# Masks, scan and PSUM banks in a two-kind transformer kernel: one mask product per head and scores first, one masked scan per direction, paired banks

## The reference, cut to what matters

```python
# first kind: RWKV-7 time mix (8 heads of 64), a pool branch, gates, feed-forward
def step(state, inp):                      # 512 steps
    r_t, w_t, k_t, v_t, kk_t, a_t = inp
    sk = jnp.einsum('bhvk,bhk->bhv', state, kk_t)
    state = (state * w_t[:, :, None, :] - sk[..., None] * (a_t * kk_t)[:, :, None, :]
             + v_t[..., None] * k_t[:, :, None, :])
    return state, jnp.einsum('bhvk,bhk->bhv', state, r_t)
mixed = br_gate[:, :, 0] * (y_a @ proj_a[l]) + br_gate[:, :, 1] * (y_b @ proj_b[l])
x = x + gt1 * (mixed @ w_out[l])
# second kind: gated linear attention in both directions (4 heads, keys 128, values 256) ...
cum = jnp.cumsum(la, axis=3)               # la = log_sigmoid(...) / 16, per chunk
q_dec, k_intra = q * jnp.exp(cum), k * jnp.exp(-cum)
# ... beside softmax attention (8 query heads, 2 key heads of 128), gates, feed-forward
pr = jax.nn.softmax(sc, axis=-1)
mixed = jax.nn.sigmoid(gate_a) * branch_a + jax.nn.sigmoid(gate_b) * branch_b
```

## Time and profile before

| | us |
|---|---|
| median of 3 runs (3934.14 to 3939.48) | 3936.67 |
| the profiled execution | 3938.62 |
| its span, first to last instruction | 3936.8 |
| PE busy | 3727.2 (95%) |
| PEld (weight loads) busy | 3017.7 (77%) |
| DVE busy | 1827.7 (46%) |
| ACT busy | 842.1 (21%) |
| POOL busy | 2269.6 (58%) |

### The profile page before, as it was taken

One profiled execution on the slowest core, in us unless ns is written; L12 is line 12 of the kernel. 1 busy time (PEld: TensorE's weight loads), 2 busy tenths in 40 slices (PEclk: granted clock), 3 DMA queues, 4 the chain that ended last, 5 costly groups with the idle time before them and its releaser, 6 DMA issues.

```text
span 3936.8 us, 53124 instructions
## 1 busy us (share of the span) xinstructions
PE 3727.2 (95%) x21300; PEld 3017.7 (77%) x21300; DVE 1827.7 (46%) x2494; ACT 842.1 (21%) x1318; POOL 2269.6 (58%) x2218
## 2 busy tenths in 40 slices
PE   5999999999999899999899999999998999999997
PEld 4777678887777678887777677888787776778886
DVE  5644653244754652125543554523465435453325
ACT  3321110005121110003321532000243225220002
POOL 4523767785523677774446356777644453567773
PEclk9999999999999999998999999999989999999998
DMA  4223445342223443332223132333322331333332
GB/s 184 83 79 107 140 144 145 118 145 73 71 79 103 142 145 109 97 97 67 65 73 121 52 99 83 97 97 97 96 62 62 95 95 57 105 83 97 97 98 65
DMA packets 192196, 386.09 MB, mean 98 GB/s; under 512 B 21456, under 2 KB 21584, under 8 KB 190288
## 3 DMA queue, kind: packets, MB, share of 16 engines
q1 hardware_dynamic: 169776, 338.24, 29.1%
q10 hardware_dynamic: 22176, 44.45, 3.2%
HBM read 361.64 MB, written 20.97 MB: 97 GB/s over the span
## 4 chain that ended last, share of the span: by engine, by line
PE 83%; DVE 10%; ACT 4%; DMA 1%; issue 1%; ACTq 0%; SPq 0%; DVEq 0%
PE psum L415 17%; PE psum L417 17%; PE psum L416 17%; PE psum L487 3%; PE psum L489 2%; PE psum L488 2%; PE psum L509 2%; PE psum L970 1%; DVE units L1849 1%; PE psum L945 1%; PE psum L603 1%; PE psum L462 1%; PE psum L593 1%; PE psum L807 1%; PE psum L809 1%
## 5 line engine op out<-in xcount | busy, mean ns | idle before, releaser
L2249 POOL TENSOR_SCALAR w_hi<-raw 128x512 fp32r<-128x512 f32 x1082 | 747.0, 690 | 1523.4 <-DMA raw<-weight_chunks 1520.5
L2251 POOL TENSOR_TENSOR w_lo<-raw,w_hi 128x512 fp32r<-128x512 f32 x1082 | 1486.7, 1374 | 90.2
L415 PE MATMUL psum<-in_hi,w_hi 128*128 128x512 f32 x1920 | 761.7, 397 | 2.9 <-ACT mg L1545 1.3
L416 PE MATMUL psum<-in_lo,w_hi 128*128 128x512 f32 x1920 | 749.3, 390 | 0.0
L417 PE MATMUL psum<-in_hi,w_lo 128*128 128x512 f32 x1920 | 749.2, 390 | 0.0
L415 PEld LDWEIGHTS psum<-in_hi,w_hi 128*128 128x128 f32 x1920 | 361.9, 188 | 90.1 <-issue 11.1
L416 PEld LDWEIGHTS psum<-in_lo,w_hi 128*128 128x128 f32 x1920 | 361.8, 188 | 80.3 <-issue 6.2
L417 PEld LDWEIGHTS psum<-in_hi,w_lo 128*128 128x128 f32 x1920 | 361.5, 188 | 76.1
L487 PE MATMUL psum<-in_hi,w_hi 128*128 128x512 f32 x576 | 255.6, 444 | 20.0 <-ACT nt L1108 10.0
L488 PE MATMUL psum<-in_lo,w_hi 128*128 128x512 f32 x576 | 227.2, 394 | 0.0
L489 PE MATMUL psum<-in_hi,w_lo 128*128 128x512 f32 x576 | 227.0, 394 | 0.0
(11 more groups left out here) (430 smaller groups left out, 6703.7 us busy)
## 6 DMA issues: line engine op xcount, KB each, us to landing
raw<-weight_chunks SPq DMA_DIRECT2D x1082, 256.0 KB, 2.6
ada_col<-ada_slabs SPq DMA_DIRECT2D x80, 512.0 KB, 4.1
spill<-gate_st ACTq DMA_DIRECT2D x56, 256.0 KB, 2.8
ada_at<-ada_slabs SPq DMA_DIRECT2D x8, 1024.0 KB, 15.8
gin<-spill ACTq DMA_DIRECT2D x32, 256.0 KB, 3.2
mgs<-spill ACTq DMA_DIRECT2D x32, 256.0 KB, 2.9
sml<-small ACTq DMA_DIRECT2D x4, 1024.0 KB, 5.6
spill<-nt ACTq DMA_DIRECT2D x16, 256.0 KB, 2.6
```

What stands on the lines that cost most here:

```text
L415: pe.matmul(bank[:], wh, hi[:, i, :], start=(i == 0), stop=False)
L416: pe.matmul(bank[:], wh, lo[:, i, :], start=False, stop=False)
L2249: ts(w_hi[:, slot, :], raw[:, slot, :], 1.0, 1.0, ALU.mult, ALU.mult).then_inc(sem("chunk_hi"), 1)
L2251: ins = tt(w_lo[:, slot, :], raw[:, slot, :], w_hi[:, slot, :].bitcast(F32), ALU.subtract)
```

## The change

- **Recurrence.** The scores come first in a chunk; the transposes `tok` 0, 1, 2 come in levels 2, 3, 4, behind the filler block. VectorE masks all 512 columns of a head in one product and computes `mt` for each half of the partitions from `units` directly; ScalarE copies the diagonal blocks to `ac`. Fillers: 0, 2, 2, 4 blocks behind the four pairs of scores in place of 6 behind all, and 1 behind `inv_t`.
- **Decays.** One scan of 512 tokens per head and direction, with a mask `keep2` of ones that is zero at the first token of each chunk. The middle value is subtracted from the scan's result directly; the exclusive sum of the backward direction is a subtraction shifted by one token and a column for the first token. `mid` and the two memsets go.
- **Banks.** Each bank has one count of uses. In both stages of the second kind of block (decays and heads; attention) projections use banks 0 and 1 ("lin2") and fillers banks 2 and 3 ("bg2"); `p2a`, `p2b` and all the rest use "lin" as before. In `gla_core` the fillers before the heads are 8, 2, 2, 8 in place of 2, 2, 2, 8.

```diff
+FILL_SCORE = (0, 2, 2, 4)
+FILL_CORE = (8, 2, 2, 8)
+        keep2 = ar("keep2", 2, [P, T])
-        mid = [ar(f"mid{i}", 94 + i / 32, [P, NCH]) for i in range(2)]
-        BANKS = {"lin": (0, 3), "bg": (3, 1), "aux": (4, 4)}
+        BANKS = {"lin": (0, 1, 2), "bg": (3,), "aux": (4, 5, 6, 7), "lin2": (0, 1), "bg2": (2, 3)}
+        uses_of = {}
...
             def begin(name, pool, order=None):
-                n = used[pool]
-                first, banks = BANKS[pool]
-                b, uses = first + n % banks, n // banks
+                b = BANKS[pool][used[pool] % len(BANKS[pool])]
+                uses = uses_of.get(b, 0)
+                uses_of[b] = uses + 1
...  (TensorE, wkv_chunk)
-                for i, src in enumerate((b_f, k_f, v_f)):
+                def token_rows(i):
...
+                pe.wait_ge(sem("wkv_in"), count("wkv_in", l))
                 for d in range(RT):
                     names = [("score", l, c, 2 * d + i) for i in range(2)]
...
+                    fill(FILL_SCORE[d])
-                fill(6)
...  (behind inv_t)
+                fill(1)
...
                     fill(2 if v == 1 else 1)
+                    if 2 <= v < 5:
+                        token_rows(v - 2)
                     pe.wait_ge(*moved(("am", l, c, v)))
...  (TensorE, block2)
-                side_jobs([(("g2a", l, m), "w_in2", l, N_GA + m) for m in range(DT)], "bg")
+                side_jobs([(("g2a", l, m), "w_in2", l, N_GA + m) for m in range(DT)], "bg2")
+                lane[0] = "lin2"
...  (ScalarE, wkv_chunk)
+                    gates_before(("score", l, c, NH - 1), gate_st)
+                    act.wait_ge(*moved(("score", l, c, NH - 1)))
+                    for k in range(2):
+                        rows = slice(HB * k, HB * k + HB)
+                        af(ac[rows, :, :], units[rows, :, 0, rows], ACT.Copy).then_inc(sem("diag_ready"), 1)
...  (VectorE, wkv_chunk)
-                    for i in range(2):
-                        ins = tt(units[:, h, 2 * i:2 * i + 2, :],
-                                 bank[:, 256 * i:256 * i + 256].rearrange("p (a t) -> p a t", a=2), pair, ALU.mult)
+                    tt(units[:, h, :, :].rearrange("p (j a) t -> p j (a t)", j=2),
+                       bank[:].rearrange("p (j t) -> p j t", j=2), pair, ALU.mult).then_inc(bank_read(job), 1)
...
-                    dve.tensor_copy(ac[rows, :, :], units[rows, :, 0, rows]).then_inc(sem("vector_step"), 1)
+                    tt(mt[rows, :, :], units[rows, :, 0, rows], compact(0, rows), ALU.mult).then_inc(sem("vector_step"), 1)
-                tt(mt[:], ac[:], compact(0), ALU.mult).then_inc(sem("vector_step"), 1)
...  (VectorE, gla_decay)
-                    for c in range(NCH):
-                        dve.tensor_tensor_scan(ln[h][i][:, c, :], kst[:, K_ONES, :], la[i][:, c, :], 0.0,
+                    ins = dve.tensor_tensor_scan(flat, keep2[:], flat, 0.0, ALU.mult, ALU.add)
+                    at = HB - 1 - i
+                    ins = tt(ln[h][i][:, :, i:P], la[i][:, :, 0:P - i],
+                             la[i][:, :, at:at + 1].to_broadcast([P, NCH, P - i]), ALU.subtract)
...
+                        ts(ln[h][1][:, :, 0], la[1][:, :, at], -1.0, None, ALU.mult).then_inc(sem("vector_step"), 1)
+                        ins = tt(dsc[h][1][:, 0:n], la[1][:, 0:n, P - 1], la[1][:, 0:n, at], ALU.subtract)
+                        ins = tt(dsc[h][1][:, 0:n], dsc[h][1][:, 0:n], la[1][:, 1:NCH, at], ALU.add)
```

More of the change, by code:

```diff
@@ L280, in emit @@
         jobs = {}
-        used = {"lin": 0, "bg": 0, "aux": 0}
+        used = {pool: 0 for pool in ("lin", "bg", "aux", "lin2", "bg2")}
         ranks = {"lin": 0, "bg": 0, "aux": 0, "late": 0}
-        BANKS = {"lin": (0, 3), "bg": (3, 1), "aux": (4, 4)}
+        BANKS = {"lin": (0, 1, 2), "bg": (3,), "aux": (4, 5, 6, 7), "lin2": (0, 1), "bg2": (2, 3)}
+        uses_of = {}
         closed = {}
@@ L320, in moved, with compact @@
             return bank_read(job), turn(job)
-        def compact(i):
+        def compact(i, rows=slice(0, P)):
             o = (K_HALF + i // 2) * P + i % 2 * HB
-            return kst[:].rearrange("p k t -> p (k t)")[:, o:o + HB].unsqueeze(1).to_broadcast([P, NH, HB])
+            part = kst[:].rearrange("p k t -> p (k t)")[rows, o:o + HB]
+            return part.unsqueeze(1).to_broadcast([rows.stop - rows.start, NH, HB])
         def half(t, b, second):
@@ L406, in linear @@
             def linear(name, blocks, hi, lo, ready):
-                bank = begin(name, "lin")
+                bank = begin(name, lane[0], "lin")
                 for i, desc in enumerate(blocks):
@@ L802, in token_major @@
                     ts_ = slice(t * P, (t + 1) * P)
-                    bank = begin(name + (t,), "lin")
+                    bank = begin(name + (t,), lane[0], "lin")
                     for k in range(DT):
@@ L838, in gla_core @@
                 v = gv[h % 2]
-                fill((2, 2, 2, 8)[h])
+                fill(FILL_CORE[h])
                 pe.wait_ge(sem("qd_ready"), count("qd_ready", (l, h)))
@@ L925, in block2 @@
                 fill(DT * DT)
+                lane[0] = "lin"
                 for m in range(DT):
@@ L928, in block2 @@
                                hi=go_hi, lo=go_lo)
-                side_jobs([(("g2b", l, m), "w_in2", l, N_GB + m) for m in range(DT)], "bg")
+                side_jobs([(("g2b", l, m), "w_in2", l, N_GB + m) for m in range(DT)], "bg2")
+                lane[0] = "lin2"
                 for i in range(KVH):
@@ L1214, in block1 @@
                 for c in range(NCH):
[L1215 to L1223, removed]
-                    flat = lambda t: t[:].rearrange("p h t -> p (h t)")
+                    flat = lambda t: t[:].rearrange("p h t -> p (h t)")
+                    gates_before(("score", l, c, NH - 1), gate_st)
[3 more added lines that the diff above has]
+                        af(ac[rows, :, :], units[rows, :, 0, rows], ACT.Copy).then_inc(sem("diag_ready"), 1)
+                        act.wait_ge(sem("diag_ready"), passed("diag_ready", (l, c)))
                     job = ("inv_t", l, c)
-                    gates_before(job, gate_st)
                     act.wait_ge(*done(job))
@@ L1235, in block1 @@
                         act.wait_ge(bank_read(job), turn(job))
+                        if 2 <= v < 5:
+                            job = ("tok", l, c, v - 2)
+                            act.wait_ge(*done(job))
+                            af(tok[v - 2][:], bank_of(job)[:], ACT.Copy).then_inc(bank_read(job), 1)
+                            act.wait_ge(bank_read(job), turn(job))
                     low, high = slice(0, HB), slice(HB, P)
@@ L1841, in wkv_chunk @@
             def wkv_chunk(l, c):
-                pair = kst[:, K_STRICT:K_INCL + 1, :]
+                pair = kst[:, K_STRICT:K_INCL + 1, :].rearrange("p a t -> p (a t)").unsqueeze(1).to_broadcast([P, 2, 2 * P])
                 for h in range(NH):
@@ L1869, in level_part @@
                     dve.wait_ge(sem("bm_ready"), passed("bm_ready", (l, c, v)))
+                dve.wait_ge(sem("diag_ready"), count("diag_ready", (l, c)))
                 level_part(1)
@@ L2117, in block2 @@
                 normed_inputs(("m1", l), cols_of(l, "g_mix_pre"))
+                for part, value in ((keep2[:], 1.0), (by_chunk(keep2[:])[:, :, 0:1], 0.0)):
+                    dve.memset(part, value).then_inc(sem("vector_step"), 1)
+                    dve.wait_ge(sem("vector_step"), passed("vector_step"))
                 for h in range(GH):
```

45 lines of the change are left out of this document (12 added, 33 removed).

## The result

The changed kernel takes 3910.7 us (median of 4 runs, 3909.2 to 3919.7) against 3937.3 of before (4 runs); the ratio is 0.9946 (0.9933 to 0.9958). By the medians that is 26.6 us faster where 49.7 were forecast, and 1.7 us outside the range. The ratio on record makes it 21 us; I can't say why the two differ. By the runs listed for this pair, what they gain on it would be 3 to 5 us smaller. The two profiled executions stand at spans of 3909.2 and 3936.8, 27.6 apart; the table splits that by TensorE's marks at the ends of the stages.

What follows compares the result with a forecast made beforehand. TensorE, busy 3727 of 3937 us, was taken as the bound, leaving at most 210 us of waits. Terms -9.8 (recurrence), -13.2 (gated stages), -17.3 (bank waits), -10.2 (`kd`), +0.8 gave -49.7: 3887 us, range 3870 to 3909.

Steps and rivals of the forecast that it cites:

- part 1: Recurrence, 8 chunks: shorter masks and earlier scores, less the price of transposes in the levels; -9.8 us, bounds -3 and -16.
- The four banks and the new fillers: Recurrence, scores with filler blocks between pairs: VectorE waits 0.8 for heads 6 and 7, `inv_t` starts 1.8 us earlier.
- the diagonal: Recurrence, before `inv_t`: two 64x512 products and the subtraction take 2.2 us instead of 2.5, copies going to ScalarE.
- part 3: Decays on VectorE: a head falls from 23 to 12 instructions, the last from 15.7 to 11.7 us beside GpSimd, 6.7 alone.
- 1.1 us of TensorE's wait for `mt` stays: Recurrence, at `inv_t`: the four blocks behind the last scores end at 223.9, `inv_t` starts at 225.1.
- clock rival: Recurrence, levels 2 to 4: transposes among small products let the clock drop to half; +19 us, 3906, chance 2%.
- a level longer than 4.3 us: Recurrence: sign that the forecast is wrong; transposes in levels 2 to 4 were charged 0.4 us a level, 1.2 a chunk.
- part 2: Gated stages: 12 blocks per layer leave the fill before `pa`, so gates are fetched 6.8 and 6.4 us earlier; -13.2 us.
- the two `gv` waits at 1.43: Block 2, heads 0 and 1: the third `gv` job waits 1.5 us for the first's bank, 3.0 a layer.
- Moved cover: Rival: blocks taken ahead of `pa` and `p2a` were needed, part 2 gives nothing, half the bank waits reappear; 3909, chance 13%.
- Scores bound by order: Rival, recurrence until `inv_t`: no gain because diagonal copies queue behind gates on ScalarE; +14 us, 3901, chance 6%.
- two-bank lane: Slower rival, block 2: ScalarE is late for each of 88 jobs using two banks; +47 us, 3984, chance 3%.

Runs made afterwards that it cites:

- fill_behind: Changed kernel with the two filler blocks between score pairs 2 and 3 moved behind pair 3: 3882.0 us, ratio 0.9867 to the kernel before.
- tok_first: Changed kernel with the 12 transposes and their ScalarE copies back at the chunk's start: 3913.6 us, ratio 0.9950 to the kernel before.
- blocks_23: Changed kernel with seven instead of four filler blocks behind score pair 3: 3898.1 us, ratio 0.9903 to the kernel before.
- blocks_17: Changed kernel with two instead of four blocks behind pair 3 and none behind `inv_t`, 17 a chunk: 3928.4 us, ratio 0.9983 to the kernel before.
- after: The profiled execution of the changed kernel, with nothing further altered: span 3909.2 us against 3936.8 for the kernel before.
- core_12: Fastest kernel (3876.6: late blocks behind pair 3, `gv` in aux banks) with four blocks moved from before `p2a` to before head 3's keys: 3878.2 us.
- banks_undone: Changed kernel with one bank for fillers and three for the rest in block 2, as before: 3917.5 us, ratio 0.9953 to the kernel before.
- decays_undone: Changed kernel with four scans per direction and the decay's 23 small instructions, as before: 3922.0 us, ratio 0.9964 to the kernel before.
- one_between: Changed kernel with one of the two blocks between score pairs 2 and 3 moved behind pair 3: 3887.0 us, ratio 0.9874 to the kernel before.

## Why the prediction was wrong

**The step that failed** is the fourth of part 1, "The four banks and the new fillers", with the fifth of its prices, the diagonal. Counted from the chunk's start, forecast against measured in chunk 1: pair 3 done at 7.2 and 7.8; heads 6 and 7 masked at 8.7 and 9.3; product, product, subtraction 2.2 and 3.4. So `inv_t` came 1.85 late. The first 0.6 is TensorE's changes between blocks and scores, where my sum had only the durations: two pairs with their blocks took 2.84 and 2.66, and 2.5 were counted for each. The other 1.2 is GpSimd: the two products take 1.71 and the subtraction 1.64 with its conversion beside them, and 1.41 and 0.69 in fill_behind without it. I had two prices for one instruction in part 3 and used the high one there alone. Over eight chunks the front cost 14 us.

**The second part of the same step** was what the delay would do. I wrote that "1.1 us of TensorE's wait for `mt` stays" and gave it no price of its own. It was 2.1, and behind it TensorE ran at half clock in four chunks, 1.5 us each, 6 us. My clock rival named the transposes as the trigger; fill_behind (transposes in the levels, no fall) and tok_first (none there, and the falls stay) clear them, and blocks_23, where blocks fill the idle time, shows that it is the idle time. The levels cost 1.4 a chunk instead of 1.2, another 2 us; the forecast's sign of a level longer than 4.3 us came in the level with `tok` 2, in six chunks of eight (4.36 to 4.56). That makes 22 us for a miss of 20; half clocks of before in layer 0's chunk 3 and at layer 1's first scores, which did not come back in full, take 3.4 off again, so the account closes to about 1.5 us. How much of the 31 us of fill_behind belongs to the conversion and how much to the clock is read from the traces; no run takes away one alone and leaves the other.

**Right.** The masks' 0.72 each and layer 1's wait of 4.43; part 2 in both layers to 0.4 us, and blocks_17 shows its cause; the two `gv` waits at 1.43; the decay at 11.3, within 0.4 of the forecast (its listed prices add up to 10.85, and the trace has 0.3 of steps between them, so the 11.7 was 0.5 too high by its own terms); `k` 0 of layer 1. Block 2 of layer 0 came out at -13.9 for -13.75, with two errors that cancel: the chain to `kd` gained nothing instead of 1.0, because the last decay's start lost 1.9, the decay won 4.4 and the keys lost 2.5. Half clock has a part in that number too, which the forecast did not have: behind the wait at `kd` it lasted 10.2 us instead of 17.1 (3.4 won), and behind head 3 came 3.4 us of it that before had not (1.7 lost). In layer 1 the stage missed by 4.4. Part of it is clock: 15.3 us are lost to half clock around the stage's start where it was 13.7 before, and 3.4 behind head 3, where before had none. No experiment was made on that; in fill_behind the same stage takes 2.8 us less than in after with the same block 2, so part of it varies by execution.

**The rivals.** "Moved cover" gives the time measured within 2 us by another mechanism: the gate's fetch did come 6.6 us earlier, and no wait took the banks' place beyond those at `gv` and at head 3. "Scores bound by order" was near in place and wrong in cause: ScalarE's diagonal copies start at once. The two-bank lane was no trouble.

## What to carry to other kernels

Where an engine feeds another through few buffers, as TensorE feeds VectorE the scores here, try the filler work behind the last feed first and not between feeds; sum the switches too, and look at what the late chain then meets. An idle time of TensorE of about 2 us can have a second price, the half clock behind it: it came in half of the cases here (1.5 us each). Filling the idle time gave back both (blocks_23), unless the blocks were needed elsewhere (core_12). And time each edit's order apart from its saving: here the saving (16 us) and the harm (31 us) were in the same stretch, and the whole hid both.

## What the runs showed of the hardware

- At `inv_t`, TensorE fell from 2.4 to 1.2 GHz around waits of 2.09 to 2.15 us in four cases of eight (after), and in five of eight each in tok_first (2.09 to 2.28), banks_undone (2.10 to 2.29) and decays_undone (2.09 to 2.18), in part in other chunks. In blocks_17 it fell in eight of eight (2.24 to 3.50), but the wait of 2.29 in banks_undone had no fall behind it, so the length of the wait does not decide it. Around waits of at most 0.25 it fell in none of 24 (fill_behind, one_between, blocks_23). A fall lasted 3.4 us, in six of blocks_17's eight 6.8.
- A 128x512 product of VectorE from two operands in SBUF takes 0.69 us alone and 1.64 beside a conversion of GpSimd; a scan of 512 takes 1.22 and 2.19. With its first operand in PSUM it took 690 to 694 ns in all 64 masks of after, 4 of which had a conversion beside them for over 0.2 us (in blocks_17 and blocks_23 11 each, with the same times). The Trainium skill ("SBUF — State Buffer", section "SBUF: two separate sides") has the two engines share ports in SBUF; the rows agree.
